# Differential heads' norm: split squares summed through a block of ones in place of column sums and spreads

## The reference, cut to what matters

```
a_d = p_d[:, :, 0] - lam * p_d[:, :, 1]
o_d = einsum('bhqk,bhkd->bhqd', a_d, v_d)
o_d = rmsnorm(o_d, subln) * (1.0 - lambda_init)     # x * rsqrt(mean(x*x, features) + 1e-5) * subln
return concatenate([o_f, o_d]) @ w_out
```

## Time and profile before

| | |
|---|---|
| median of 3 runs | 2677.72 us |
| profiled execution | 2677.59 us, its span 2675.7 us |
| PE busy | 2663.5 us, 12806 matmuls |
| DVE busy | 1391.0 us (52%) |
| ACT busy | 1001.1 us (37%) |
| POOL busy | 181.0 us (7%) |
| mixer steps of layer 0 / layer 1 | about 408 to 600 us / 1391 to 1583 us |
| granted TensorE clock | 1.0 |

### The profile page before, as it was taken

The page is one execution under the profiler, slowest core; times in us unless marked ns, Lnnn a source line. Parts: engine busy times, 40 slices in busy tenths (PEclk is TensorE's granted clock), DMA queues, the critical chain, the costliest instruction groups (busy, mean ns, idle before and its releaser), DMA issues.

```text
span 2675.7 us, 33948 instructions
## 1 busy us (share of the span) xinstructions
PE 2663.5 (100%) x12806; PEld 2191.3 (82%) x12806; DVE 1391.0 (52%) x1939; ACT 1001.1 (37%) x1560; POOL 181.0 (7%) x134
## 2 busy tenths in 40 slices
PE   8999999999999999999999999999999999999999
PEld 7888887888888888888888888888887888888887
DVE  5444258765444245443268665444245557834443
ACT  4222235444223233222145543222135553334553
POOL 0000024101000010000043111000000000010000
PEclk9999999999999999999999999999999999999999
DMA  4222233113223222322332112222322222323111
GB/s 161 94 94 100 96 102 95 56 40 102 94 95 101 94 94 96 101 94 94 102 103 79 56 57 97 99 94 95 101 80 79 79 79 91 103 96 98 58 66 59
DMA packets 70328, 239.20 MB, mean 89 GB/s; under 512 B 8528, under 2 KB 10832, under 8 KB 70224
## 3 DMA queue, kind: packets, MB, share of 16 engines
q1 hardware_dynamic: 69792, 236.91, 26.8%
q10 hardware_dynamic: 432, 0.87, 0.1%
HBM read 230.15 MB, written 2.10 MB: 87 GB/s over the span
## 4 chain that ended last, share of the span: by engine, by line
PE 97%; DVE 1%; ACT 0%; DVEq 0%; issue 0%; DMA 0%; ACTq 0%; SPq 0%
PE bank L394 22%; PE bank L396 21%; PE bank L395 21%; PE score L394 5%; PE score L395 5%; PE score L396 5%; PE flip_bank L394 2%; PE flip_bank L396 2%; PE flip_bank L395 2%; PE score L1126 1%; PE flip_bank L1148 1%; PE score L1840 1%; PE bank L2662 1%; PE score L2630 1%; PE bank L2557 1%; PE score L2634 0%
## 5 line engine op out<-in xcount | busy, mean ns | idle before, releaser
L377 DVE TENSOR_TENSOR w_lo<-w_raw,w_hi 128x1024 fp32r<-128x1024 f32 x427 | 527.2, 1236 | 545.9 <-ACT w_hi L337 534.9
L394 PE MATMUL bank<-h_hi,w_hi 128*128 128x512 f32 x1856 | 741.9, 400 | 0.5 <-DVE w_lo L377 0.5
L396 PE MATMUL bank<-h_hi,w_lo 128*128 128x512 f32 x1856 | 724.0, 390 | 0.0
L395 PE MATMUL bank<-h_lo,w_hi 128*128 128x512 f32 x1856 | 723.2, 390 | 0.0
L337 ACT ACTIVATE w_hi<-w_raw 128x1024 fp32r<-128x1024 f32 x427 | 447.9, 1051 | 426.3 <-DMA w_raw<-stream 421.1
L396 PEld LDWEIGHTS bank<-h_hi,w_lo 128*128 128x128 f32 x1856 | 348.7, 188 | 74.3
L394 PEld LDWEIGHTS bank<-h_hi,w_hi 128*128 128x128 f32 x1856 | 349.0, 188 | 72.7 <-issue 4.0
L395 PEld LDWEIGHTS bank<-h_lo,w_hi 128*128 128x128 f32 x1856 | 349.3, 188 | 70.1 <-issue 2.4
L533 ACT ACTIVATE hid_hi<-tmp 128x512 f32 (+1 forms) x88 | 55.6, 632 | 409.6 <-DVE tmp L737 409.6
L731 DVE TENSOR_TENSOR tmp<-bank,rstd 128x512 f32<-128x512 f32 x132 | 91.1, 691 | 148.4 <-PE bank L396 148.1
L394 PE MATMUL score<-h_hi,w_hi 128*128 128x512 f32 x384 | 149.5, 389 | 0.0
(11 more groups left out here) (523 smaller groups left out, 3888.6 us busy)
## 6 DMA issues: line engine op xcount, KB each, us to landing
w_raw<-stream SPq DMA_DIRECT2D x427, 512.0 KB, 3.3
tmp<-tmp SPq DMA_DIRECT2D x64, 64.0 KB, 2.0
x_tok<-x SPq DMA_DIRECT2D x4, 512.0 KB, 6.4
wx_raw<-stream SPq DMA_DIRECT2D x4, 512.0 KB, 4.7
out<-out_tok SPq DMA_DIRECT2D x8, 256.0 KB, 2.0
tmp<-qr SPq DMA_DIRECT2D x16, 64.0 KB, 2.1
tab_in_f<-tables SPq DMA_DIRECT2D x1, 704.0 KB, 10.3
cos_sin<-rope ACTq DMA_DIRECT2D x1, 512.0 KB, 4.2
```

Of the source, the lines that this page charges most:

```text
L377: nc.vector.tensor_tensor(w_lo[:, s, :], w_raw[:, s, :], w_hi[:, s, :].bitcast(F32), ALU.subtract).then_inc(lo_ready, 1)
L394: nc.tensor.matmul(dst, whi, xhi, start=start, stop=False)
L395: nc.tensor.matmul(dst, whi, xlo, start=False, stop=False)
L396: return nc.tensor.matmul(dst, wlo, xhi, start=False, stop=stop)
```

## The change

The squares of a differential head are written to d_sq (two buffers) and split on the spot: ACT copies the high half to d_sq_hi, DVE subtracts for d_sq_lo, both in block 2. In block 3 PE sums both through ones_r, a 128x128 block of ones in fp32r, by two matmuls of 512 columns into bank7, where each partition then has the sum of every token. ACT copies it to d_var in block 0 of the next step (head 3: takes the root directly), and at step 20 takes the root of the other three, 1536 columns. The reciprocal is now 128x512 for each head and stands with the multiply in steps 21, 22, 25 and 26 (normed_at), where the spreads' steps were 22, 23, 26 and 27. The spreads, the copies of d_stat and their waits go. ones_r is filled once at the start.

```diff
-        def spread_at(k):
-            return {4 * 5 + 2: 0, 4 * 5 + 3: 1, 4 * 6 + 2: 2, 4 * 6 + 3: 3}.get(k)
+        def normed_at(k):
+            return {4 * 5 + 1: 0, 4 * 5 + 2: 1, 4 * 6 + 1: 2, 4 * 6 + 2: 3}.get(k)
...
                     if b == 2 and 1 <= g <= DIFF_HEADS:
                         act.wait_ge(d_out, DIFF_HEADS * layer + g)
-                        nc.scalar.activation(d_squares[:, g - 1, :], d_raw[:, g - 1, :], ACT.Square).then_inc(d_sq, 1)
+                        if g >= 3:
+                            act.wait_ge(d_ss, DIFF_HEADS * layer + g - 2)
+                        nc.scalar.activation(d_sq[:, (g - 1) % 2, :], d_raw[:, g - 1, :], ACT.Square)
+                        act.drain()
+                        nc.scalar.activation(d_sq_hi[:, g - 1, :], d_sq[:, (g - 1) % 2, :],
+                                             ACT.Copy).then_inc(d_squared, 1)
+                    if b == 0 and 2 <= g <= DIFF_HEADS + 1:
+                        act.wait_ge(d_ss, DIFF_HEADS * layer + g - 1)
+                        ins = nc.scalar.activation(d_var[:, g - 2, :], bank[7][:, :],
+                                                   ACT.Copy if g <= DIFF_HEADS else ACT.Sqrt,
+                                                   scale=1.0 / P, bias=0.0 if g <= DIFF_HEADS else small[:, 0:1])
+                        ins.then_inc(d_var_in, 1)
...
                     if (g, b) == (DIFF_HEADS + 1, 0):
-                        act.wait_ge(d_stat_in, DIFF_HEADS * (layer + 1))
-                        nc.scalar.activation(d_stat[:, :], d_stat[:, :], ACT.Sqrt, scale=1.0 / P,
+                        nc.scalar.activation(d_var[:, 0:DIFF_HEADS - 1, :], d_var[:, 0:DIFF_HEADS - 1, :], ACT.Sqrt,
                                              bias=small[:, 0:1]).then_inc(d_root, 1)
...
+                    if b == 2 and 1 <= g <= DIFF_HEADS:
+                        dve.wait_ge(d_squared, DIFF_HEADS * layer + g)
+                        nc.vector.tensor_tensor(d_sq_lo[:, (g - 1) % 2, :], d_sq[:, (g - 1) % 2, :],
+                                                d_sq_hi[:, g - 1, :].bitcast(F32), ALU.subtract).then_inc(d_split, 1)
+                    h = normed_at(k)
+                    if h is not None:
+                        dve.wait_ge(d_root, layer + 1)
+                        nc.vector.reciprocal(d_var[:, h, :], d_var[:, h, :])
+                        dve.drain()
+                        nc.vector.scalar_tensor_tensor(
+                            out=d_raw[:, h, :], in0=d_raw[:, h, :], scalar=lam[:, 6 + layer:7 + layer], in1=d_var[:, h, :],
+                            op0=ALU.mult, op1=ALU.mult).then_inc(d_norm, 1)
                     if b == 1 and g > DIFF_HEADS:
                         pair_low(g - 1 - DIFF_HEADS)
-                    if b == 3 and 1 <= g <= DIFF_HEADS:
-                        dve.wait_ge(d_ss, DIFF_HEADS * layer + g)
-                        nc.vector.tensor_copy(d_stat[:, TB * (g - 1):TB * g], bank[7][:, 0:TB]).then_inc(d_stat_in, 1)
-                    if (g, b) == (DIFF_HEADS + 1, 1):
-                        dve.wait_ge(d_root, layer + 1)
-                        nc.vector.reciprocal(d_stat[:, :], d_stat[:, :]).then_inc(d_inverse, 1)
-                    h = spread_at(k)
-                    if h is not None:
-                        dve.wait_ge(d_spread, DIFF_HEADS * layer + h + 1)
...
                 def diff_sums(h):
-                    pe.wait_ge(d_sq, DIFF_HEADS * layer + h + 1)
-                    for b in range(TB):
-                        ins = nc.tensor.matmul(bank[7][:, b:b + 1], d_squares[:, h, P * b:P * b + P], ones[:, 0:1],
-                                               start=True, stop=True)
-                    ins.then_inc(d_ss, 1)
-
-                def diff_spread(h):
...
+                    pe.wait_ge(d_squared, DIFF_HEADS * layer + h + 1)
+                    nc.tensor.matmul(bank[7][:, :], ones_r[:, :], d_sq_hi[:, h, :], start=True, stop=False)
+                    pe.wait_ge(d_split, DIFF_HEADS * layer + h + 1)
+                    nc.tensor.matmul(bank[7][:, :], ones_r[:, :], d_sq_lo[:, h % 2, :], start=False,
+                                     stop=True).then_inc(d_ss, 1)
...
-                    if spread_at(k) is not None:
-                        diff_spread(spread_at(k))
```

More of the change, by code:

```diff
@@ L182, in build @@
         o_lo = place("o_lo", [P, KT, S], F32R)
-        d_squares = place("d_squares", [P, DIFF_HEADS, S], at=O_AT + 4 * S * 4)
+        d_sq_hi = place("d_sq_hi", [P, DIFF_HEADS, S], F32R, at=O_AT + 4 * S * 4)
+        d_var = place("d_var", [P, DIFF_HEADS, S], at=O_AT + 4 * S * 4)
+        d_sq = place("d_sq", [P, 2, S], at=O_AT + 4 * S)
+        d_sq_lo = place("d_sq_lo", [P, 2, S], F32R, at=O_AT + 4 * S)
         d_raw = place("d_raw", [P, DIFF_HEADS, S], at=O_AT + 4 * S * (KT + 4))
@@ L188, in build @@
         cum_part = place("cum_part", [8, S], BF16, at=O_AT)
+        ones_r = place("ones_r", [P, P], F32R, at=arena_bytes - 5 * P)
         v_feat = sqsum
@@ L244, in build @@
         mixed = sem("mixed")
-        d_out, d_sq, d_ss, d_stat_in, d_root, d_norm = (
-            sem(n) for n in ("d_out", "d_sq", "d_ss", "d_stat_in", "d_root", "d_norm"))
-        d_inverse, d_spread = sem("d_inverse"), sem("d_spread")
+        d_out, d_squared, d_ss, d_var_in, d_root, d_norm = (
+            sem(n) for n in ("d_out", "d_squared", "d_ss", "d_var_in", "d_root", "d_norm"))
+        d_split = sem("d_split")
         od_half, od_ready, of_half, of_ready = (sem(n) for n in ("od_half", "od_ready", "of_half", "of_ready"))
@@ L644, in mixer @@
                         exps(k)
-                    h = spread_at(k - 1)
+                    h = normed_at(k - 1)
                     if h is not None:
@@ L918, in mixer @@
                         nc.vector.tensor_copy(d_raw[:, g - 1, :], bank[7][:, :]).then_inc(d_out, 1)
+                    if b == 2 and 1 <= g <= DIFF_HEADS:
[10 more added lines that the diff above has]
+                            op0=ALU.mult, op1=ALU.mult).then_inc(d_norm, 1)
                     if b == 1 and g > DIFF_HEADS:
                         pair_low(g - 1 - DIFF_HEADS)
-                    if b == 3 and 1 <= g <= DIFF_HEADS:
-                        dve.wait_ge(d_ss, DIFF_HEADS * layer + g)
-                        nc.vector.tensor_copy(d_stat[:, TB * (g - 1):TB * g], bank[7][:, 0:TB]).then_inc(d_stat_in, 1)
-                    if (g, b) == (DIFF_HEADS + 1, 1):
-                        dve.wait_ge(d_root, layer + 1)
-                        nc.vector.reciprocal(d_stat[:, :], d_stat[:, :]).then_inc(d_inverse, 1)
-                    h = spread_at(k)
-                    if h is not None:
-                        dve.wait_ge(d_spread, DIFF_HEADS * layer + h + 1)
-                        nc.vector.scalar_tensor_tensor(
-                            out=d_raw[:, h, :], in0=d_raw[:, h, :], scalar=lam[:, 6 + layer:7 + layer], in1=bank[7][:, :],
-                            op0=ALU.mult, op1=ALU.mult).then_inc(d_norm, 1)
                 flip_low(NSTEP - 1)
@@ L953, in _ @@
             nc.vector.memset(small[:, 2:3], NORM_EPS * RMS_EPS).then_inc(small_ready, 1)
+            nc.vector.memset(ones_r[:, :].bitcast(F32), 1.0)
             def x_copy(m):
@@ L1156, in mix @@
                     if 1 <= g <= DIFF_HEADS:
-                        pe.wait_ge(d_stat_in, DIFF_HEADS * layer + g)
+                        pe.wait_ge(d_var_in, DIFF_HEADS * layer + g)
                     if g > DIFF_HEADS:
                         pe.wait_ge(of_ready, GROUPS // 2 * layer + g - DIFF_HEADS)
-                        pe.wait_ge(d_norm, DIFF_HEADS * layer + min(2 * (g - DIFF_HEADS), DIFF_HEADS))
                     if g in (DIFF_HEADS, DIFF_HEADS + 1):
```

## The result

The changed kernel takes 2696.09 us (median of 4 executions, 2695.01 to 2698.08) where the one before took 2677.84 (4 executions, 2677.71 to 2678.09) beside it: ratio 1.0070, 95% interval 1.0057 to 1.0083. It is 18.3 us slower. The forecast was 2686, a slowdown of 8.5 us, in a range that ended at 2694. The direction is right, and the time lies 2.1 us above the range. The profiled execution took 2696.96 us, with a span of 2695.1 and a mean granted clock of 0.995, where the kernel before had 1.0.

What follows compares the result with a forecast made beforehand. PE, 97% of the chain of waits, was taken as the bound, with DVE close behind in places. Waits +4.6 and sums -0.35 make 4.25 us a layer, 8.5 for two; 2677.6 + 8.5 gives 2686 us, range 2680 to 2694.

Steps and rivals of the forecast that it cites:

- rival (1): PE's stops before steps 24 and 28 lower its clock: +5 to +10 us, 2691 to 2696 us; chance 0.17.
- The waits: Steps 21 to 28: reciprocals delay DVE's maxima, then k_lo and PE's scores of steps 24 and 28: +1.4 + 3.2 = +4.6 us a layer.
- The signs named for it: Two k_lo waits a layer, about 2.7 us each; step 23's maxima 4.4 us after its scores; steps after 28 unchanged.
- The sums: Steps 6 to 19: DVE's subtractions put PE 0.7 us behind in step 13; by the end -0.3 to -0.4 us a layer.
- The overlap of GpSimd and DVE: Step 7: w_lo took 1.74 us for the usual 1.2 beside POOL's k_lo; started 0.68 later it misses that.
- What PE saves: Four sums at 0.5 us and four spreads at 1.1 us a layer: 6.4 us off PE, if nothing else gave way.
- Rival (2): The chain around k_lo and step 12 gives back 2.2 us more a layer: +4 us, 2680 to 2683; chance 0.22.
- Rival (3): Steps 22 and 26: with a reciprocal under about 1.2 us PE's order decides, 2668 or 2665 us; chance 0.06.
- Rival (4): The change isn't what it says, for instance late roots: bound ACT's 2 us in step 20; no chance of its own.

Runs made afterwards that it cites:

- after: The changed kernel itself, reciprocals of 128x512 on DVE included, against the kernel before: 2696.09 us, ratio 1.0070.
- e3_fill: The changed kernel with useless matmuls filling PE's stops around the flips of steps 23 and 27: 2686.11 us, 1.0033 to the kernel before.
- e1_no_recip: The changed kernel without its eight reciprocals and the drains behind them, the norm's factor left out: 2677.34 us, 1.0000 to the kernel before.
- e7_lnexp: The changed kernel with the factor made on ACT by Ln and Exp, no reciprocal on DVE: 2677.01 us, 0.9999 to the kernel before.
- e8_khi_first: e7_lnexp with ACT making q_hi and k_hi ahead of the differential heads' o_hi: 2671.53 us, 0.9979 to the kernel before.
- e4_before_recips: The kernel before plus a useless 128x512 reciprocal at the end of DVE's steps 22 and 26: 2683.91 us, 1.0026.
- e12: The changed kernel with reciprocal and multiply in steps 21, 24, 25 and 27: 2682.90 us, 1.0021 to the kernel before.
- e2: The changed kernel with the reciprocals on 256 of the 512 columns: 2685.86 us, 1.0030 to the kernel before.
- e10: The changed kernel, reciprocals kept, with the differential heads' o_hi behind q_hi and k_hi on ACT: 2691.16 us, 1.0053 to the kernel before.
- e13: The changed kernel with useless matmuls only behind the flips of steps 23 and 27: 2687.74 us, 1.0038 to the kernel before.

## Why the prediction was right or wrong

**The step that failed** is the one that set rival (1) at 0.17 with "Against it: the stops are shorter than that one". It compared stops of up to 2.8 us with the one of 6.92 us at the kernel's start and took it for likely that short ones do nothing, with no row for a short one. In after the clock fell at all four places. Its size had been worked out well: about 2.5 us a stop, 5 to 10 us and a time of 2691 to 2696 stand in the rival, and 1.56, 2.88, 2.39 and 2.55 us in the trace, 9.5 us by e3_fill and 2696.09 were measured. What was wrong was its chance, and so the centre and the upper end of the range, which left out the upper half of that rival. The Trainium skill ("TensorE: Matmul & The Clock Gate", Part 1) was cited there for idleness as what brings TensorE back to 1.2 GHz; the four falls agree with that in direction.

**The waits**, which the forecast rested on, were right. Reciprocal 3.34 us (3.35 forecast), drain and multiply until 544.41 (544.4), k_lo's end at 549.77 (549.7), scores at 549.83 (549.75; layer 0 of this run starts 0.28 later, so from the layer's start it is 0.2 us earlier than forecast). e3_fill, where the clock is out of it, has +4.4 us a layer against 4.25 forecast, of which 3.2 between steps 24 and 28 (forecast 3.2). The signs named for it came: two waits for k_lo a layer, 2.55 and 2.76 us (2.7), the maxima of step 23 4.20 us behind its scores (4.4), step 23 9.62 and 9.63 us long (9.8), step 27 11.45 (11.6). One sign failed: the steps after 28 were to keep their old lengths, and step 28 itself grew by 2.39 and 2.55 us, as step 24 did by 1.56 and 2.88. That is the clock.

**The sums** were mis-sized in the middle and right at the end. PE was to be 0.7 us behind in step 13 and is 0.37 and 0.29; pt_lo came 0.72 late (0.87 forecast). More than half of the difference is a slip in reading: the earlier trace rows show the flip's weight load at 477.33, which runs ahead of its matmul, and the matmul itself started at 477.56. The earlier trace rows were read the same way (454.33, where the matmul started at 454.45), and PE is 0.12 and 0.05 behind at step 9 where 0.25 had been worked out. The overlap of GpSimd and DVE was judged rightly: w_lo of step 7, now started at 448.52, as k_lo ends, took 1.22 us and not 1.74. At step 20 PE is at -0.29 and -0.37, with -0.35 forecast.

**What PE saves** was taken too large, unnoticed because the waits cover it. A spread gives back 0.9 us (step 22 to 23: -0.25 to -1.15) and not 1.1, and a sum 0.32 to 0.38 (step 7 to 8: -0.32) and not 0.5: the two matmuls of step 7 hold PE for 0.64 us (449.64 to 450.28), nearer the 0.6 that was named beside the 0.46. That is 5 us a layer and not 6.4.

**Rival (2)**, that the chain gives back more, did not come: k_lo took 1.55 and 1.76 us (1.56 and 1.77 before). **Rival (3)** put PE's whole saving at 2665 to 2668, were the reciprocal gone. e1_no_recip and e7_lnexp show 2677 instead, of which some 1 to 2 us are the loss in the later layer. That rival took it that without the reciprocal k_lo would be ready; in fact k_lo is then the next to be late, behind o_hi on ACT, and with that mended too (e8_khi_first) the kernel gets to 2671.5. **Rival (4)** is out: the roots were in time, for DVE was idle 0.0 us before the eight reciprocals.

## What to carry to other kernels

Where one engine is busy 97% of the chain, ask of every instruction that a change puts on another engine what stands behind it in that engine's order, and not how busy the engine is on average: two reciprocals a layer on a half idle DVE cost 6.6 us in e4_before_recips. Add to each new stop of PE the clock that it may lose: in the profiled executions it fell at 15 of the 22 places with a stop of 1.6 us or more, for 1.3 to 2.9 us each. And a wait that is taken away shows the next link of its chain: only reciprocal and ACT's order together brought the time under that of the kernel before.

## What the hardware showed beyond what was expected

Short stops can bring TensorE's clock to 1.2 GHz, but not each time. The places in the mixer layers where PE had stopped for 1.5 us or more (us, read in layer 0; the step is the one whose scores come late, and for e12 the one in which PE stops), and by how much the growth of the steps behind exceeds that of the waits:

| stop | kernel, step | layer 0 | layer 1 |
|---|---|---|---|
| 1.60 | e1, 28 | 0 | +1.3 |
| 1.60 | e7, 28 | 0 | 0 |
| 1.59 | e2, 24 | 0 | +1.6 |
| 1.88 | e4, 28 | +1.35 | +1.3 |
| 1.91 | e10, 24 | 0 | +1.5 |
| 2.07 | e13, 28 | 0 | +1.3 |
| 2.55 | after, 24 | +1.6 | +2.9 |
| 2.77 | e2, 28 | +2.8 | +1.3 |
| 1.82 and 1.77 | e10, 28 | +2.6 | +2.6 |
| 2.07 and 2.76 | after, 28 | +2.4 | +2.6 |
| 3.41 | e12, 28 | 0 | +1.4 |

The last row forbids a rule by the stop's length alone: the longest single stop left the clock up in layer 0, and stops of half its length brought it down. A fall costs 1.3 to 2.9 us, and the price goes with the moment at which the clock falls. In nine of the fifteen falls it came down 0.5 to 1.7 us after PE had started again; these cost 1.3 to 1.6 us. In the other six it came down while PE still stood, 0.15 to 1.0 us before the start, and these cost 2.4 to 2.9 us; half speed lasted about twice as long in them. Step 24 of after has one of each kind (windows of 10 us from PE's start, layer 0, then layer 1; the granted clock is 0.83 and 0.68):

```profile
549.83:559.83 10.00, 10.00 (x56) 8.15 (x57) 5.04 (x12) 3.82 (x12) 0.00 (x0) 0.83 0.01 1
1541.43:1551.43 10.00, 10.00 (x50) 8.20 (x51) 3.72 (x10) 2.84 (x7) 0.00 (x0) 0.68 0.00 0
```

With two stops close together it fell 4 times of 4. The Trainium skill ("TensorE: Matmul & The Clock Gate", Part 1) says of a kernel's start that the number of slow matmuls varies between runs of the same kernel; the equal stops with unequal outcomes may be of that kind, which no run here shows. The ten executions of e12_placed differ too: the fastest (2679.75 us) has a mean clock of 0.999, the three slowest (2683.84 to 2684.50) 0.997. What decides between equal stops stays open.

ACT's exponential of 128x512 took 628 ns and DVE's reciprocal of the same tile 3343, so the way over the logarithm is 2.7 us shorter for each head and lies on ACT, which is busy 38% of the span of after, where DVE is busy 53%.
